# Moving the sample group's compressed branch and block ranking into the prompt attention's steps, and five buffers for its key and value units

## The chip, the cores and the metric

The kernel runs on one core of one Trainium2 chip. That core has five engines: TensorE (PE; its weight loads are shown apart as PEld), VectorE (DVE), ScalarE (ACT), GpSimd (POOL) and SyncE (SP), and 16 DMA engines that all queues share. The metric is the device time of one launch in microseconds. The kernel before takes 2581.03 us (median of three runs, 2580.56 to 2582.22).

## The reference

The reference is one inference step through two layers for two groups of tokens: a prompt of 512 tokens and a sample group of 8 sequences with 4 new tokens each, which have 2048 past tokens in 16 pages of a paged cache. Layer 0 mixes tokens by sparse attention in three branches, layer 1 by a Mamba-2 scan; each is followed by a SwiGLU. Cut to the attention of layer 0:

```python
lc = einsum(qg, kc) * scale - slopes * dist_c          # compressed branch: 127 blocks of the past
pc = masked_softmax(lc);  o_c = einsum(pc, vc)
imp = pad(pc.sum(heads of the group))                  # importance of the compressed blocks
p_slc = chunk sums of imp, 64 tokens a block           # 32 blocks of the past per query
score = where(forced, FORCE_SCORE, where(visible, p_slc, -1));  sel = top_k(score, 16)
ls = einsum(qg, k_sel) * scale - slopes * dist_s       # selected branch: only the chosen blocks
o_s = masked_softmax(ls) @ v_sel
o_w = windowed attention over the last 512 tokens      # window branch
o = gate0 * o_c + gate1 * o_s + gate2 * o_w;  y = o @ w_out;  x = x + y
```

The selected branch of the sample group can't be masked before the compressed branch has been ranked.

## The kernel before

All data is float32. SBUF is one hand-laid arena and PSUM eight banks of 512 columns. The program is a list of phases; each engine has its own instruction stream per phase, written out by hand with semaphores, and at the end of a phase all engines meet (`meet`). Nothing reorders the streams: the order in the code is the order on each engine.

Phase 3 (`p3_*`) is the prompt's attention. It walks 32 steps `s`: four query tiles `i` of 128 tokens, eight head pairs each. With tile `i` the keys have 128 (i+1) columns. In a step PE computes scores of step s (L1091, banks 0 to 3), turns the weights of step s-2 (L1109, banks 4 and 5), and multiplies values of step s-3 (L1129). DVE biases the scores of step s out of PSUM (`bias`, L1262), then scales the weights of step s-1 (`scale`, L1277). ACT takes the turned weights (L1192) and does the exponentials (L1184). The prompt's compressed branch for the next tile is inserted at steps k = 3 to 7 of each tile (`cmp_scores`, `cmp_bias`, `cmp_turn`). During phase 3 SP and POOL load the first key unit pair and the first value unit pair of the sample group, which then lie still.

Phase 4 (`p4_*`) is the sample group's attention. It treats the 8 sequences as four pairs. A unit is one sequence's selected keys or values: 16 pages of 128 KB, each one DMA whose source page is read from a table (`p4_load_unit`: page numbers into registers L1357, the DMAs L1360). There are four buffers for units: two for keys, two for values. SP loads the even sequence of a pair, POOL the odd one. The window is a 1 MB tile per sequence, keys and values in one DMA (L1380).

At its start phase 4 first copies the sample's queries into a block-diagonal form (L1536 to L1541), does the compressed scores of all pairs (L1393), their softmax on DVE and ACT, the importance (a product with `same_gt`, L1476, and the sums), and then ranks the 30 free blocks of each pair by comparing all with all: per pair five DVE instructions over 30x30 = 900 columns and a small one (L1567 to L1572). `sc_sel` is raised when the last pair is ranked. POOL waits for it and adds the chosen blocks' mask to the bias of 2048 columns (`comb`, L1621), SP waits for it before the second window tile, since the ranking's scratch lies there. PE waits for it before `turn(0)`.

Then PE runs, for each pair: `turn(pr)` (transposes of the weights, L1446), `scores(pr+1)` (L1405), `values(pr)` (L1458), `turn_out(pr)` (L1472), `win_scores(pr+1)` (L1421). DVE biases (L1590, L1592) once the mask of the pair is there, ACT does the exponentials (L1504, L1507), DVE sums the three branches (L1603 to L1605). SP's order in a pair: key unit after `ss_mm` (scores done), value unit after `ss_pv` (values done), then both window tiles after `ss_pv`. POOL's order: mask, key unit after `ss_mm`, value unit after `ss_pv`.

Phase 5 (`p5_*`) is the output projection: four units of seven products (L339), with weights in the four-slot ring, the first two of them needed at once. POOL forms sums of weight blocks (L385 to L392), and right before that issues one DMA that copies the whole window cache from DRAM to DRAM (`out_win`, L1629). The result is added to the residual `xT` (L1691), which stays in SBUF from the start of the kernel.

## Time and profile before

| | us |
|---|---|
| median of three runs | 2581.03 |
| the profiled execution, whole | 2581.04 |
| its span in the trace | 2579.6 |
| phase 3, the prompt's attention | about 610.1 to 836.65 |
| phase 4, the sample's attention | 836.65 to about 1046.4 |
| of it up to the last pair's ranking | 836.65 to 872.4 |
| ends of the pairs' value products | 904.3, 953.3, 1001.3, 1044.2 |

The whole execution is 1.4 us longer than its span. PE is busy 89% of the span. The times of phases are read off the timeline, by the first and last instruction of each. A busy DVE or PE in a stretch tells only that an instruction ran; the chain of waits tells which of them the end hung on.

### The profile page before, as it was taken

To read this page: it belongs to the slowest core of one execution; us is meant where nothing else is said; L and a number is where in the kernel's file an instruction comes from. 1 tells how busy PE (TensorE), PEld (TensorE's weight loads), DVE (VectorE), ACT (ScalarE), POOL (GpSimd) and SP (SyncE) were. 2 spreads that over 40 slices of the span, in tenths; PEclk is the share of its full clock that TensorE was granted. 3 is DMA by queue.
4 is the path that set the end of the run, shared out by engine and by line. 5 is a ranking of instruction groups with operands and counts; after the bars stand their busy time and mean duration, and the time that the engine had idled before them with its cause. 6 is when DMAs were issued, how large, how long until landed. Compare 5 with 4: busy or idle time off the path is not lost.

```text
span 2579.6 us, 34400 instructions
## 1 busy us (share of the span) xinstructions
PE 2288.9 (89%) x12318; PEld 1809.7 (70%) x12318; DVE 1284.4 (50%) x2112; ACT 513.9 (20%) x1205; POOL 785.0 (30%) x656
## 2 busy tenths in 40 slices
PE   7998999996788323899998999999877899999899
PEld 6866888775556211788886888788544687888687
DVE  5436333322566501555575226877667536557522
ACT  2101111113566111111110003232354001111000
POOL 4300000003000143534332424555364335433232
PEclk9988999996799665999999999999788899999999
DMA  4224333314000367521211221222132121121122
GB/s 157 83 77 126 98 99 98 86 54 141 3 1 4 125 202 266 202 82 66 98 66 45 90 112 68 71 83 84 69 129 99 53 95 66 66 98 66 47 89 80
DMA packets 86010, 234.92 MB, mean 91 GB/s; under 512 B 11121, under 2 KB 60402, under 8 KB 70610
## 3 DMA queue, kind: packets, MB, share of 16 engines
q1 hardware_dynamic: 78818, 202.84, 22.3%
q0 software_dynamic: 7024, 29.90, 3.5%
q8 instruction: 99, 1.62, 0.3%
q14 instruction: 69, 0.57, 0.1%
HBM read 216.23 MB, written 23.73 MB: 93 GB/s over the span
## 4 chain that ended last, share of the span: by engine, by line
PE 58%; DVE 9%; ACT 2%; issue 2%; SPq 2%; DMA 2%; POOL 2%; DVEq 0%; POOLq 0%; ACTq 0%
PE ps L339 46%; PE ps L1091 2%; DMA sbuf<-win 1%; PE ps L1129 1%; SPq L1360 1%; PE ps L1109 1%; POOL sbuf L2695 1%; PE ps L460 1%; ACT sbuf L1192 1%; ACT sbuf L1184 1%; PE ps L1458 1%; DVE sbuf L2078 1%; PE ps L1066 1%; DVE sbuf L2595 1%; PE ps L2268 1%
## 5 line engine op out<-in xcount | busy, mean ns | idle before, releaser
L339 PE MATMUL ps<-sbuf 128*128 128x272 f32 x6048 | 1406.5, 395 | 49.1 <-DVE sbuf L1836 19.4
L339 PEld LDWEIGHTS ps<-sbuf 128*128 128x128 f32 x6048 | 1156.4, 192 | 297.6 <-DVE sbuf L1836 20.3
L385 POOL TENSOR_TENSOR sbuf<-sbuf 128x512 f32<-128x512 f32 (+2 forms) x90 | 136.9, 1521 | 710.7 <-PE ps L339 631.1
L358 ACT ACTIVATE sbuf<-ps 128x272 f32<-128x272 f32 x180 | 71.5, 397 | 1104.4 <-PE ps L339 1075.4
L367 DVE TENSOR_TENSOR sbuf<-sbuf,ps 128x272 f32<-128x272 f32 x90 | 39.4, 438 | 246.4 <-PE ps L339 245.5
L392 POOL TENSOR_TENSOR sbuf<-sbuf 128x512 f32<-128x512 f32 (+2 forms) x90 | 145.2, 1613 | 8.1 <-PE ps L339 1.3
L389 POOL TENSOR_TENSOR sbuf<-sbuf 128x512 f32<-128x512 f32 (+2 forms) x90 | 140.0, 1556 | 7.1
L386 POOL TENSOR_TENSOR sbuf<-sbuf 128x512 f32<-128x512 f32 (+2 forms) x90 | 138.6, 1540 | 7.1
L788 PE MATMUL ps<-sbuf 128*128 128x256 f32 (+1 forms) x512 | 120.8, 387 | 2.9 <-DVE sbuf L905 2.9
L800 PE MATMUL ps<-sbuf 128*128 128x256 f32 (+1 forms) x512 | 120.0, 385 | 0.0
L794 PE MATMUL ps<-sbuf 128*128 128x256 f32 (+1 forms) x512 | 120.0, 385 | 0.0
L788 PEld LDWEIGHTS ps<-sbuf 128*128 128x128 f32 x512 | 95.2, 188 | 21.6 <-issue 4.8
L794 PEld LDWEIGHTS ps<-sbuf 128*128 128x128 f32 x512 | 96.2, 188 | 18.6
L800 PEld LDWEIGHTS ps<-sbuf 128*128 128x128 f32 x512 | 96.0, 188 | 18.6
L376 DVE TENSOR_TENSOR sbuf<-sbuf 128x272 f32<-128x272 f32 x90 | 105.5, 1172 | 3.1
L373 DVE TENSOR_TENSOR sbuf<-sbuf,ps 128x272 f32<-128x272 f32 x90 | 39.4, 438 | 131.1 <-PE ps L339 130.5
L945 DVE TENSOR_TENSOR sbuf<-sbuf,ps 128x256 f32<-128x256 f32 (+1 forms) x32 | 13.8, 430 | 180.3 <-PE ps L794 180.2
L369 DVE TENSOR_TENSOR sbuf<-sbuf,ps 128x272 f32<-128x272 f32 x90 | 39.3, 437 | 125.8 <-PE ps L339 125.0
L996 POOL DMA_DIRECT2D sbuf<-sbuf x16 | 9.8, 618 | 289.4 <-PE ps L788 273.0
L1421 PE MATMUL ps<-sbuf 128*32 128x512 f32 x32 | 7.7, 1058 | 99.4 <-DMA sbuf<-win 99.4
L1831 DVE TENSOR_TENSOR sbuf<-sbuf 128x544 f32<-128x544 f32 x88 | 93.0, 1056 | 3.0
L1262 DVE CUSTOM_DVE_ANT_0 sbuf<-ps,sbuf 128x128 f32<-128x128 f32 (+3 forms) x128 | 57.4, 490 | 52.1 <-PE ps L1091 47.6
(349 smaller groups left out, 2541.5 us busy)
## 6 DMA issues: line engine op xcount, KB each, us to landing
sbuf<-w_gu SPq DMA_DIRECT2D x44, 1024.0 KB, 5.9
sbuf<-cmp_pages SPq DMA_DIRECT2D x256, 128.0 KB, 2.3
sbuf<-w_down SPq DMA_DIRECT2D x32, 704.0 KB, 5.3
sbuf<-w_ssd_in SPq DMA_DIRECT2D x20, 1024.0 KB, 4.8
sbuf<-w_nsa_in SPq DMA_DIRECT2D x10, 1024.0 KB, 4.9
sbuf<-sel_k SPq DMA_DIRECT2D x64, 128.0 KB, 6.5
sbuf<-sel_k POOLq DMA_DIRECT2D x64, 128.0 KB, 5.6
sbuf<-sel_v SPq DMA_DIRECT2D x64, 128.0 KB, 4.3
```

What stands on the lines that cost most here:

```text
L339: last = pe.matmul(ps[:, bank_of(u, j), 0:HALF], a[:, kt * P:(kt + 1) * P], b[:, kt], start=kt == 0, stop=kt == kts - 1)
L358: do(act.activation(dst, bank_in(u, j), ACT.Copy), f_copied)
L376: do(dve.tensor_tensor(c1[:, n1], c1[:, n1], p4, ALU.add))
L385: do(pool.tensor_tensor(sv[:, 0], a21, a22, ALU.add), f_sums)
L386: do(pool.tensor_tensor(sv[:, 1], sv[:, 0], a11, ALU.subtract), f_sums)
L389: do(pool.tensor_tensor(sv[:, 2], a11, a21, ALU.subtract), f_sums)
L392: do(pool.tensor_tensor(sv[:, 3], a12, sv[:, 1], ALU.subtract), f_sums)
L788: last = pe.matmul(shared, ws[:, kt, hs], rows[:, kt, :, :, 1], start=kt == 0, stop=kt == KT - 1)
L794: last = pe.matmul(odd, w1(kv, 1, kt)[:, hs], e[:, kt], start=kt == 0, stop=kt == KT - 1)
L800: last = pe.matmul(even, w1(kv, 0, kt)[:, hs], d[:, kt], start=kt == 0, stop=kt == KT - 1)
L1262: dve.tensor_tensor_reduce(S_ring[:, n % S_BUFS, 0:w], ps[:, x, 0:w], cn_("dist")[:, SEQ - w:SEQ], -float(slope[head_of(gp * 4 + r, x % 2) ...
L1831: do(dve.tensor_tensor(c[:, x], c[:, x], rstd, ALU.mult), g_took if v % 2 == 0 else None)
```

## The change

Four edits go together.

1. The queries' copy, the compressed branch and the ranking move from the start of phase 4 into steps of phase 3. They use bank 4 between `turn(s-2)` and `values(s-3)` of a step, and the spent `xT` and parameter regions as scratch. The scores of the compressed branch are done at step 8, the exponential too, the weights on DVE at step 9, importance and block sums at step 10, the transposes at step 16, and the ranking in 16 parts at steps 12 to 27, four per pair. PE waits at `turn(s-1, 0)` of the next step until bank 4 has been read.
2. Units have five places (`a` to `e`), used in turn; `e` is `xT`. The first key unit of pair 1 is loaded in phase 3 (by SP, once the ranking is done).
3. PE does `values(pr)` and `turn_out(pr)` ahead of `scores(pr+1)`. SP loads a value unit after `ss_mm`, the window's key halves after `sw_mm`, its value halves after `ss_pv`, then the next key unit. POOL loads the odd key unit, then forms the mask, then loads the odd value unit.
4. `xT` is loaded again from DRAM at the start of phase 5, and DVE waits for it in unit 0. Two of the four weight slots are loaded after it, at `ss_pv` of the last pair; two after that of the third.

```diff
+        def sc_scores(pe, s):
+            sc_bank_free(pe, s)      # pe.wait_ge(a_pt, 4 * (s - 2) + 3)
+            pe.wait_ge(s_diag, 4)
+            for pr in range(PAIRS):
+                for bb, gp in QUARTERS:
...
+                    last = pe.matmul(ps[rows32(bb, gp), 4, pr * NC:(pr + 1) * NC], q_diag[gp][:, b], kcT[:, b, gp],
+        def sc_importance(pe, s):
...
+            pe.wait_ge(sc_dve, SC_DVE["weights"])
+            pe.matmul(ps[:, 4, 0:PAIRS * NC], cn_("same_gt"), weights_c.rearrange("p i n -> p (i n)"), start=True,
...
+        def sc_bias(dve, do):        # three instructions of 508 columns; sc_weights: four, one of them small;
+            dve.wait_ge(sc_pe, SC_PE["scores"])                # sc_blocks: three
...
+        def sc_rank(dve, do, pr, part):
...
+            if part == 0:
+                do(dve.tensor_tensor(above, other, mine, ALU.is_gt))
+            elif part == 1:
+                do(dve.tensor_tensor(equal, other, mine, ALU.is_equal))
+            elif part == 2:
+                dve.wait_ge(cn_in, 48)
+                do(dve.tensor_tensor(equal, equal, lower, ALU.mult))
+                do(dve.tensor_tensor(above, above, equal, ALU.add))
+            else:
+                do(dve.tensor_reduce(rank, above, AX.X, ALU.add))
+                do(dve.tensor_scalar(sel_bias[:, pr, 1:NBLK - 1], rank, TAKE - 0.5, NEG, ALU.is_gt, ALU.mult),
...
@@ p3_pe: turn(s, x)
+                if x == 0 and s + 1 == SC_SCORES:
+                    pe.wait_ge(sc_dve, SC_DVE["bank_read"])
+                if x == 0 and s + 1 == SC_IMPORTANCE:
+                    pe.wait_ge(sc_dve, SC_DVE["importance_read"])
...
@@ p3_dve, at the end of a step
+                if s == 4:
+                    sc_queries(dve, do)
+                if s == SC_SCORES:
+                    sc_bias(dve, do)
+                if s == SC_SCORES + 1:
+                    sc_weights(dve, do)
+                if s == SC_IMPORTANCE:
+                    sc_blocks(dve, do)
+                if SC_RANK <= s < SC_RANK + 4 * PAIRS:
+                    sc_rank(dve, do, (s - SC_RANK) // 4, (s - SC_RANK) % 4)
@@ p4_sp
+            p4_load_unit(sp, "K", 0)
+            p4_load_unit(sp, "V", 0)
+            sp.wait_ge(sc_dve, SC_DVE["blocks"])
+            sp.dma_start(lower.rearrange("p s o -> p (s o)"), t["const_n"][:, CONST_N["lower"]]).then_inc(cn_in, 16)
+            sp.wait_ge(sc_dve, SC_DVE["chosen"])
+            sp.wait_ge(sc_act, SC_ACT["turned_taken"])
+            p4_load_unit(sp, "K", 2)
...
+            sp.wait_ge(met, 12)
+            win_part(0, k_half, wk_in)
+            sp.dma_start(ali, t["const_ali"]).then_inc(late_in, 16)
+            rest = slice(CN_P3, CONST_N["lower"].start)
+            sp.dma_start(cn[:, rest], t["const_n"][:, rest]).then_inc(late_in, 16)
+            win_part(0, v_half, wv_in)
+            for pr in range(PAIRS - 1):
+                sp.wait_ge(ss_mm, pr + 1)
+                p4_load_unit(sp, "V", 2 * pr + 2)
+                sp.wait_ge(sw_mm, pr + 1)
+                win_part(pr + 1, k_half, wk_in)
+                sp.wait_ge(ss_pv, pr + 1)
+                win_part(pr + 1, v_half, wv_in)
+                if pr + 2 < PAIRS:
+                    p4_load_unit(sp, "K", 2 * pr + 4)
@@ p4_pe
             for pr in range(PAIRS):
                 turn(pr)
-                if pr + 1 < PAIRS:
-                    scores(pr + 1)
                 values(pr)
                 turn_out(pr)
                 if pr + 1 < PAIRS:
+                    scores(pr + 1)
                     win_scores(pr + 1)
@@ p4_pool
+            mask(0)
+            for pr in range(PAIRS - 1):
+                pool.wait_ge(ss_mm, pr + 1)
+                p4_load_unit(pool, "K", 2 * pr + 3)
+                pool.wait_ge(ss_s, pr + 1)
+                mask(pr + 1)
+                pool.wait_ge(ss_pv, pr + 1)
+                p4_load_unit(pool, "V", 2 * pr + 3)
@@ p5_sp
-            sp.wait_ge(ss_mm, PAIRS)
-            ring_rounds(sp, "nsa_out", 4)
+            sp.wait_ge(ss_pv, PAIRS - 1)
+            for i in range(2):
+                sp.dma_start(ring[:, (s0 + i) % RING], t["w_nsa_out"][i]).then_inc(w_in[(s0 + i) % RING], 16)
+            sp.wait_ge(ss_pv, PAIRS)
+            sp.dma_start(xT, t["x"]).then_inc(x_in, 16)
+            for i in range(2, 4):
+                sp.dma_start(ring[:, (s0 + i) % RING], t["w_nsa_out"][i]).then_inc(w_in[(s0 + i) % RING], 16)
```

## Rows read from the trace of the kernel before

**Rows 1.** Chain that ended last, by line, 836 to 1052 us.

```profile
by line: DMA sbuf<-win 16.4%; SPq L1360 12.5%; issue 10.6%; PE ps L1458 9.5%; SPq L1357 6.7%; PE ps L1405 6.6%; PE ps L1446 5.0%; DVE sbuf L1592 3.2%; DMA sbuf<-sel_k 3.0%; PE ps L1421 2.7%; DVE sbuf L1569 2.1%; DVE sbuf L1570 2.1%; DVE sbu
```

**Rows 2.** Stretches: length, busy per engine, granted PE clock, DMA share, GB/s.

```profile
694.00:836.65 142.65, 123.36 (x1148) 88.23 (x1148) 89.43 (x282) 95.17 (x265) 0.00 (x0) 0.96 0.01 1
836.65:872.40 35.75, 8.98 (x86) 3.88 (x86) 31.05 (x41) 1.23 (x2) 0.35 (x2) 0.64 0.21 81
904.30:953.30 49.00, 17.12 (x263) 10.55 (x263) 5.07 (x15) 6.80 (x15) 21.12 (x33) 0.62 0.64 215
```

**Rows 3.** The same chain in order of time (start, length), pair 1's cycle.

```profile
904.32 0.97 SPq L1357
...
918.94 12.56 DMA sbuf<-win
...
934.50 2.28 DVE sbuf L1592 x2
...
939.70 3.96 PE ps L1446 x17
943.66 4.43 PE ps L1405 x32
...
948.22 5.08 PE ps L1458 x184
```

**Rows 4.** Timeline of PE and DVE before and in the ranking.

```profile
844.31 2.06 PE L1476 MATMUL ps<-sbuf 128*128 128x508 f32 x2 [4.76 <-DVE sbuf L1552]
...
846.48 0.69 DVE L1557 COPY sbuf<-ps 128x508 f32<-128x508 f32 x1 [0.83 <-PE ps L1476]
...
848.91 1.10 DVE L1567 TENSOR_TENSOR sbuf<-sbuf 128x900 f32<-128x900 f32 x1
```

**Rows 5.** DVE, first bias of steps 9, 14, 17, 27; brackets: idle before.

```profile
677.13 0.43 DVE L1262 CUSTOM_DVE_ANT_0 sbuf<-ps,sbuf 128x256 f32<-128x256 f32 x1 [0.22 <-PE ps L1091]
...
709.28 0.43 DVE L1262 CUSTOM_DVE_ANT_0 sbuf<-ps,sbuf 128x256 f32<-128x256 f32 x1 [2.21 <-PE ps L1091]
...
724.67 0.56 DVE L1262 CUSTOM_DVE_ANT_0 sbuf<-ps,sbuf 128x384 f32<-128x384 f32 x1 [0.67 <-PE ps L1091]
...
792.58 0.69 DVE L1262 CUSTOM_DVE_ANT_0 sbuf<-ps,sbuf 128x512 f32<-128x512 f32 x1 [1.17 <-PE ps L1091]
```

**Rows 6.** Two stretches of 10 us, columns as in group 2.

```profile
690.00:700.00 10.00, 7.43 (x44) 5.72 (x45) 7.38 (x21) 3.51 (x11) 0.00 (x0) 0.67 0.00 0
...
1020.00:1030.00 10.00, 1.94 (x8) 0.23 (x8) 1.64 (x7) 0.45 (x1) 0.00 (x0) 0.50 1.02 417
```

**Rows 7.** POOL's timeline in pair 1: value unit, mask, key unit.

```profile
909.70 9.31 POOL L1360 DMA_DIRECT2D sbuf<-sel_v  x16 [22.21 <-issue]
919.03 3.63 POOL L1621 TENSOR_TENSOR sbuf<-sbuf 128x2048 f32<-128x2048 f32 x1
924.23 9.31 POOL L1360 DMA_DIRECT2D sbuf<-sel_k  x16 [1.58 <-issue]
```

**Rows 8.** DMA issues with median us to landing; the first of 836.6:872, then 904.3:953.

```profile
sbuf<-const_n SPq DMA_DIRECT2D x1, 770.0 KB, 6.3
...
sbuf<-win SPq DMA_DIRECT2D x2, 1024.0 KB, 11.1
sbuf<-sel_k POOLq DMA_DIRECT2D x16, 128.0 KB, 5.8
```

**Rows 9.** The copy `out_win`; a load issued beside it (1060.5); queues 1068:1072.

```profile
out_win<-win POOLq DMA_DIRECT2D x1, 28.5
...
sbuf<-w_gu SPq DMA_DIRECT2D x1, 1024.0 KB, 18.0
...
q0 software_dynamic: 16, 1.05, 77.0%
q1 hardware_dynamic: 16, 0.13, 9.1%
```

**Rows 10.** The chain after phase 4: all products of the output projection.

```profile
1052.31 51.86 PE ps L339 x224
```

More of the change, by code:

```diff
@@ L1006, in build @@
         top[0] = att_base
-        cn = region(CONST_N["own_head"].start)
+        cn = region(CONST_N["lower"].start)
         cn_ = lambda name: cn[:, CONST_N[name]]
@@ new lines, in sc_importance, with sc_turn @@
+        def sc_importance(pe, s):
+            sc_bank_free(pe, s)
+            pe.wait_ge(sc_dve, SC_DVE["weights"])
+            pe.matmul(ps[:, 4, 0:PAIRS * NC], cn_("same_gt"), weights_c.rearrange("p i n -> p (i n)"), start=True,
+                      stop=True).then_inc(sc_pe, 1)
+        def sc_turn(pe, s):
+            sc_bank_free(pe, s)
+            pe.wait_ge(sc_dve, SC_DVE["gated"])
+            for pr in range(PAIRS):
+                last = pe.transpose(ps[0:NC, 4, pr * P:(pr + 1) * P], Sc4[:, pr], ident)
+            last.then_inc(sc_pe, 1)
@@ L1332, in build @@
-        above = PT.rearrange("p j n -> p (j n)")[:, 512:512 + FREE_BLOCKS ** 2].rearrange("p (s o) -> p s o", s=FREE_BLOCKS)
-        equal = win[:, 1, 0:FREE_BLOCKS ** 2].rearrange("p (s o) -> p s o", s=FREE_BLOCKS)
-        dead_kv = kvT_flat[:, 0:8 * NT]
-        UNIT = [ring[:, 0:2].rearrange("p s n -> p (s n)"), ring[:, 2:4].rearrange("p s n -> p (s n)"),
-                hT_flat[:, 0:4096], dead_kv[:, 0:4096]]
-        K_of = [UNIT[b].rearrange("p (i g n) -> p i g n", i=NPAGE, g=2) for b in range(2)]
@@ L1338, in build, with place @@
-        V_of = [UNIT[2 + b].rearrange("p (i n) -> p i n", i=NPAGE) for b in range(2)]
+        dead_kv = kvT_flat[:, 0:8 * NT]
+        UNIT = {"a": ring[:, 0:2].rearrange("p s n -> p (s n)"), "b": ring[:, 2:4].rearrange("p s n -> p (s n)"),
+                "c": hT_flat[:, 0:4096], "d": dead_kv[:, 0:4096], "e": xT_flat[:, 0:4096]}
+        PLACE = {"K": (("a", "b"), ("e", "a"), ("d", "e"), ("c", "d")), "V": (("c", "d"), ("b", "c"), ("a", "b"), ("e", "a"))}
+        def place(kind, b):
+            return PLACE[kind][b // 2][b % 2]
@@ L1342, in build @@
-        win_in = [sem("win0_in"), sem("win1_in")]
+        unit_in = {(kind, b): sem(f"sel_{kind}{b}_in") for kind in "KV" for b in range(4)}
+        wk_in, wv_in = sem("win_k_in"), sem("win_v_in")
         win_stored = sem("win_stored")
-        s_diag = sem("q_diag_done")
-        sc_mm, sc_s, sc_e, sc_w, sc_imp, sc_t, sc_pt, sc_sel = [sem(f"sample_cmp_{n}") for n in (
-            "scores", "biased", "exp", "weights", "importance", "turned", "turned_taken", "selected")]
         s_comb = sem("sample_mask_done")
@@ L1360, in p4_load_unit @@
                 sp.dma_start(dst[:, i:i + 1], src[bass.ds(page, 1)].rearrange("o p n -> p o n")
-                             ).then_inc(unit_in[x], 16)
+                             ).then_inc(unit_in[kind, b % 4], 16)
         def p4_sp(sp):
             sp.wait_ge(w_used, slot_at["w1"] + 4)
-            for pr in range(PAIRS):
-                for x in (0, 2):
-                    if pr >= 1:
-                        sp.wait_ge(ss_mm if x < 2 else ss_pv, pr)
-                    p4_load_unit(sp, x, 2 * pr)
-                if pr == 0:
-                    sp.wait_ge(met, 12)
-                    sp.dma_start(ali, t["const_ali"]).then_inc(late_in, 16)
-                    rest = slice(CN_P3, CONST_N["lower"].stop)
-                    sp.dma_start(cn[:, rest], t["const_n"][:, rest]).then_inc(late_in, 16)
-                for b in range(2):
-                    if pr >= 1 and b == 0:
-                        sp.wait_ge(ss_pv, pr)
-                    if pr == 0 and b == 1:
-                        sp.wait_ge(sc_sel, 1)
-                    sp.dma_start(win[:, b], t["win"][2 * pr + b]).then_inc(win_in[b], 16)
+            p4_load_unit(sp, "K", 0)
@@ L1397, in scores @@
             def scores(pr):
-                for x in range(2):
-                    pe.wait_ge(unit_in[x], 16 * NPAGE * (pr + 1))
+                for bb in range(2):
+                    pe.wait_ge(*unit_there("K", 2 * pr + bb))
                 if pr >= 1:
@@ L1472, in turn_out @@
                 pe.transpose(ps[:, 7, 0:P], o_rows, ident).then_inc(ss_ot, 1)
-            pe.wait_ge(sc_w, 1)
-            pe.matmul(ps[:, 6, 0:PAIRS * NC], cn_("same_gt"), weights_c.rearrange("p i n -> p (i n)"), start=True,
-                      stop=True).then_inc(sc_imp, 1)
-            pe.wait_ge(sc_w, 2)
-            for pr in range(PAIRS):
-                last = pe.transpose(ps[0:NC, 7, pr * P:(pr + 1) * P], Sc4[:, pr], ident)
-            last.then_inc(sc_t, 1)
             scores(0)
@@ L1688, in p5_dve @@
                 sum_products(dve, dve_do, U_NSA_OUT + i, seven_regs, c[:, 0], c[:, 1])
+                if i == 0:
+                    dve.wait_ge(x_in, 32)
                 for x in range(2):
```

201 lines of the change are left out of this document (108 added, 93 removed).

## The prediction

> **What bounds the kernel now.** I read four views, in this order. The first is the chain that ended last in the stretch of the sample's attention [rows 1]. Its largest shares are no arithmetic: 16.4% waits for window data, 12.5% is SP issuing DMAs (L1360), 6.7% is SP reading page numbers (L1357). The stretches say the same: from 904.3 to 953.3, one pair, PE is busy 17.12 of 49 us and VectorE 5.07, and the DMA engines move 215 GB/s; in the first 35.75 us VectorE is busy 31.05 us and PE 8.98 [rows 2]. So the stage has two parts with different limits, 35.7 us of the compressed branch and ranking on VectorE, then four pairs paced by a queue. The third view, the chain in order of time, shows how a pair is paced [rows 3]: after the values SP reads page numbers, issues 16 value pages and only then the window (904.32 to 918.94, 14.6 us), the window lands 12.56 us later, and only then come window scores, bias (2.28), exponential, turns (3.96), scores of the next pair (4.43) and values (5.08). The fourth is VectorE's timeline in the prompt's steps, which says how much room the moved work finds [rows 5].
>
> **The change part by part, phase 4.** I count from the start of phase 4, which lies at 836.65. Before, the last pair's values end at 1044.2, so at 207.6.
>
> *Pair 0.* Key units of pair 0 are there, so its scores end at about 6 (5 us and a start). The mask waits for constants: key halves, `ali` and the rest are 2.33 MB, where before 1.75 MB had landed 6.7 us after the start (issue 0.4 us in, 6.3 us to land [rows 8]); 0.58 MB more at the 417 GB/s of a full stretch [rows 6] is 1.4 us, so 8.1. Mask 3.63 [rows 7] gives 12 with POOL's start. VectorE's two small biases and 2.28 of L1592 give 15.5, the exponential 2.2 more, 17.8. Turns, with the last take, 4.6; 22.4. Values 5.08 [rows 3]: 27.7. The four pairs' first values before ended at 67.7 (904.3). This removes the ranking (35.7) and the wait for pair 1's key unit, which held up values(0) because its scores came first.
>
> *Pairs 1 to 3.* Two cycles compete. The arithmetic of a pair: sum of branches and `turn_out` 2, scores 4.4 to 5.7 (5.5 taken), window scores 2, biases 3.1, exponential 2.2, turns 4.5, values 5.2: 24.6 us [rows 3]. POOL's queue: it reads page numbers for 5.4 us (904.32 to 909.70), issues for 9.31, the mask takes 3.63, and the next unit's page numbers are read beside the mask, as before (mask at 919.03, first DMA at 924.23, 5.2 us later) [rows 3, 7]. In the new order that is key unit 14.6, mask and value unit 14.5: 29.1 us for a pair. A page lands 5.8 us after its issue [rows 8]. Laid out: first key unit of POOL (K3) issued 13.5 to 22.8, landed 28.5, in time for scores(1) at 29.7; its value unit V3 starts at values(0) done, 27.7, and lands at 48; turns(1) are done at 46.6, so values(1) run 48 to 53.2. K5 is issued 47.6 to 56.9 and lands at 62.5: scores(2) wait for it from 55. Values(2) end at 84.9. K7 is issued 76.6 to 85.9 and lands at 91.5: scores(3) wait again, 91.5 to 97; then 2, 3.1, 2.2, 4.5 and 5.2 give values(3) done at **114**. SP issues 13 to 14 us for a unit, two units and four window halves a pair, 29 us too, but each of its transfers is wanted later than POOL's, and I give it nothing. The window, which paced the stage, lands ahead: its key halves for pair 2 are issued at about 57 for window scores at 68, against 11.1 us to land [rows 8].
>
> The stage gives back 207.6 - 114 = **93.6 us**. Bounds: if POOL's queue didn't count, 27.7 + 3 x 24.6 = 101.5 (gain 106); if the unit landings in the two waits and the window's were all as slow as the 11.1 us of a window tile, another 5 on each of two waits and on one value unit, 129 (gain 79). I take the layout by rows, nearer to the first since 31 MB in 114 us are 290 GB/s, below the 417 of a full stretch [rows 6].
>
> **Phase 3, what is added.** A step here is a loop of scores, bias, turns and values, in which VectorE's idle time before the next bias says what fits. At steps 8 to 10 it is 0.22 us or less [rows 5]: nothing fits. Step 8: PE's compressed scores take 1.1 and VectorE waits for them, then three instructions of 0.71 over 508 columns; the next bias starts at 679.8 for 677.13, +2.65. Step 9: 3 x 0.71 + 0.2 = +2.4. Step 10: importance is 2.06 on PE [rows 4], VectorE waits, three of 0.71 follow, +3.1. Sum 8.1. The four query copies at step 4 (1.0) lie in an idle gap behind the prompt's compressed branch: 0.
> The ranking's parts are 1.13, 1.13, 2.26 and 1.32 us (L1567 is 1.10 [rows 4]). At steps 12 to 15 and 20 to 23 the gaps are 1.8 to 3.1 (one of 2.21 stands in [rows 5]), since the prompt's own inserts hold PE: only about 0.6 remains, where step 19's part sits in front of step 20's bias. The gap that step 16 leaves is 0.67, the two after it are 0.41 and 0.73, the one of step 26 is 1.17 [rows 5]: the excess is 0.5 + 0.7 + 1.5 + 0.3 (step 25) + 1.1 = 4.1. The transposes at step 16 (four of about 0.27 on PE and a take on ScalarE) are not hidden, PE leads there: 1.2. Sum 5.9. The clock: PE's granted clock was 0.67 in the 10 us after the prompt's own inserted work [rows 6], which is a mean over stretches at 1.2 and at 2.4 GHz. Inserted VectorE work makes PE idle in the same way at steps 8 to 10, so I add 2 us, two steps at the lower level, each about 1 us longer. Phase 3: **+16**. Bounds: nothing below 8 (steps 8 to 10 have no cover), and 36, if no added instruction found room (31 on VectorE, 4 on PE, 1 on ScalarE).
>
> **Phase 5, what is moved.** Before, all four weight slots were issued at 1015.9, 28 us ahead of the last values. Now `xT` (2.2 MB) and slots 2 and 3 are issued when values(3) end, and 2.4 us later POOL issues the window copy. Beside that copy a 1 MB load took 18.0 us to land, and in 1068 to 1072 the software queue moved 1.05 MB and the hardware queue 0.13 [rows 9]. So little passes until the copy lands, 28.5 us after its issue [rows 9]. About 0.8 MB go ahead of it, `xT` lands some 22 us after the last values, slot 2 at 35, slot 3 at 37. `xT` was first used 18 us after them, but VectorE may be late there while PE has banks free. A product is 51.86 / 28 = 1.85 us [rows 10], a unit 13 us, so PE wants slot 2 at 30.3 and slot 3 at 43: a stall of **+5**. Bounds 0 (the copy starts later or gives way) and 12 (all of `xT` waits for the copy, then slot 2).
> The Trainium skill's page "DMA: Bandwidth & Descriptors", section "Queues, rings and completion order", says each DMA engine takes turns between its queues, one packet at a time. The trace agrees in kind: 16 packets each, 1.05 MB against 0.13. By that rule with 17 KB packets of `xT` the stall is the one above; by the page's fit of 2 us plus bytes at 436 GB/s, which knows no second queue, it would be nought and the time 5 us less.
>
> **Sum.** Profiled execution 2581.04 (0.01 from the median): 2581.0 - 93.6 + 16 + 5 = 2508.4. I forecast **2508 us**.
>
> **The rivals.**
> *A: POOL's queue isn't late.* Units land sooner or arithmetic is slower than thought, and pairs take 24.6 us: 101.5 for 114, so 2496. For it: waits at K5 and K7 of only 7 and 5 us. Against: POOL's 9.31 us were the same in both units shown. 13%.
> *B: The two queues hold each other up.* SP's and POOL's units overlap nearly all the time now, each at some 225 GB/s (128 KB in 0.58 us [rows 7]), together above the 417 of [rows 6]; landings as slow as 11.1 us: 129 for 114, and 2523. 13%.
> *C: The ranking finds no room.* VectorE's parts delay bias, exponentials and takes in turn, and phase 3 grows by 36, not 16: 2528. Against: idle gaps of over 2 us in eight of sixteen steps. 7%.
> *D, the other side: the clock.* If VectorE's inserts let PE idle so that it is granted 1.2 GHz through steps 8 to 31, its 123.4 busy us [rows 2] up to double. That costs up to 105 and, with the 2 us above taken out, the kernel ends at 2611. It decides, against the gain of 73, from 70% of these steps at the lower level. Against: the clock was back at full after such a drop within 20 us, three times. 2%.
> *E: The window copy gives way*, the stall of phase 5 is 0 and the rest as forecast: 2503; it lies in the forecast's own range.
>
> **How the numbers follow.** The forecast with E has 65%, A 13%, B 13%, C 7%, D 2%. The range to leave out 2 in 10 takes in A's and B's centres and ends before their far sides: 2490 to 2528. A measurement of this kernel can tell 0.2%, 5 us, from no change. All cases but D are faster by 50 us or more; for mechanisms I haven't seen I leave 2% for no change and 3% for slower with D's share in it. Faster 95%.
>
> **What would show it.** Right: phase 3 longer by 16, half of it at steps 8 to 10; phase 4's first instruction a 512-column score, first values done 28 us in, last at 114; PE waiting for `sel_k` pages of POOL before scores(2) and scores(3), and no wait for `win`; a wait of some 5 us for a slot at output unit 2. Wrong: pairs longer than 32 us with SP in the chain; granted clock below 0.9 over steps 12 to 31; phase 3 growing by more than 25.

## The result, and the profile after

| | before | after |
|---|---|---|
| median, us (range) | 2581.62 (2580.56 to 2587.92, 4 runs) | 2513.71 (2511.26 to 2515.15, 4 runs) |
| ratio, 95% interval | 1 | 0.9731 (0.9713 to 0.9749) |
| profiled execution; its span | 2581.04; 2579.6 | 2514.76; 2512.8 |
| phase 3, its first PE instruction to the start of phase 4 | 226.6 | 244.0 |
| phase 4 start to last values | 207.6 | 115.6 |
| ends of the pairs' values, from its start | 67.7, 116.7, 164.7, 207.6 | 29.0, 57.0, 88.2, 115.6 |
| last values to the first product of the next stage (L460) | 59.8 | 65.7 |

The kernel is 67.9 us faster, 2.7%. The forecast was 2508, the range 2490 to 2528. The spans differ by 66.8 us, and the table accounts for it: -92.0 in phase 4, +17.5 in phase 3, +5.9 behind the last values; +1.4 come from the stages ahead of phase 3 and +0.4 from those behind L460, which the change does not touch. The start of phase 3 lies between 609.9 and 612.7 us in all the traces here, whichever kernel runs, so these two are no effect of the change.

The first view of the kernel after is the same as [rows 2], one stretch for each pair and two behind them: length, busy time and count for PE, PEld, DVE, ACT, POOL, granted PE clock, share of the DMA engines, GB/s.

```profile
855.50:884.40 28.90, 15.37 (x262) 10.33 (x262) 4.08 (x12) 6.15 (x11) 16.37 (x20) 0.76 0.89 303
884.40:911.00 26.60, 15.76 (x220) 11.19 (x223) 5.07 (x15) 6.81 (x15) 15.16 (x28) 0.74 0.80 264
911.00:940.00 29.00, 16.21 (x195) 9.79 (x191) 5.08 (x15) 6.81 (x15) 21.59 (x35) 0.71 1.05 357
940.00:971.00 31.00, 20.14 (x391) 13.80 (x383) 5.07 (x15) 6.81 (x15) 14.41 (x21) 0.83 0.80 291
971.00:979.20 8.20, 6.05 (x18) 4.31 (x18) 6.87 (x7) 0.95 (x5) 5.54 (x4) 0.79 0.96 374
```

VectorE's 31.05 us at the start of the stage [rows 2] are gone (4.08 in the first stretch). PE is busy 15.4 to 20.1 us in a pair's stretch (17.12 before), DVE the same 5.07, but in 27 to 31 us instead of 49, and the DMA engines move 264 to 357 GB/s, not 215. The arithmetic did not get shorter; what stood around it did.

The waits in phase 4 (engine and line, what it waited for, us in total, times, longest) say what is late now:

```profile
PE ps L1543 <- DMA sbuf<-sel_k: 7.6, 2, 5.5
...
PE ps L1591 <- DMA sbuf<-sel_v: 6.3, 2, 4.2
...
PE ps L1556 <- DMA sbuf<-win: 1.9, 1, 1.9
```

The window, 16.4% of the chain in [rows 1], costs 1.9 us. In its place are key and value units. POOL's timeline (start, length, instruction, count, idle before) shows whose:

```profile
904.22 9.32 POOL L1500 DMA_DIRECT2D sbuf<-sel_k  x16 [5.09 <-issue]
913.55 3.62 POOL L1701 TENSOR_TENSOR sbuf<-sbuf 128x2048 f32<-128x2048 f32 x1
918.37 5.22 POOL L1500 DMA_DIRECT2D sbuf<-sel_v  x9 [1.19 <-issue]
...
932.79 9.31 POOL L1500 DMA_DIRECT2D sbuf<-sel_k  x16 [4.80 <-issue]
942.12 3.63 POOL L1701 TENSOR_TENSOR sbuf<-sbuf 128x2048 f32<-128x2048 f32 x1
949.37 9.31 POOL L1500 DMA_DIRECT2D sbuf<-sel_v  x16 [3.63 <-issue]
```

POOL has hardly a gap but the reading of page numbers: 932.79 - 904.22 = 28.6 us from key unit to key unit, forecast 29.1. Only the last idle time, 3.63 us for 1.19 a pair earlier, is longer, since that value unit had to wait for values(2). All four waits of PE end within 0.3 us of the landing of the last page of a unit of POOL's (904.65, 919.42, 947.21 and 965.46); SP's units had landed before. PE's timeline in the same two pairs (of before: the durations in [rows 3]):

```profile
919.51 5.47 PE L1543 MATMUL ps<-sbuf 128*32 128x512 f32 x32 [5.54 <-DMA sbuf<-sel_k]
...
947.30 5.23 PE L1543 MATMUL ps<-sbuf 128*32 128x512 f32 x32 [2.06 <-DMA sbuf<-sel_k]
...
955.46 0.63 PE L1567 MATMUL ps<-sbuf 128*128 128x128 f32 x4 [1.95 <-ACT sbuf L1625]
...
959.64 3.98 PE L1578 MATMUL ps<-sbuf 128*128 128x128 f32 x17 [3.44 <-ACT sbuf L1635]
965.74 5.23 PE L1591 MATMUL ps<-sbuf 127*32 127x128 f32 x184 [2.12 <-DMA sbuf<-sel_v]
...
973.24 5.62 PE L339 MATMUL ps<-sbuf 128*128 128x272 f32 x16 [0.70 <-ACTq L251]
979.10 22.27 PE L339 MATMUL ps<-sbuf 128*128 128x272 f32 x96 [0.25 <-DVE sbuf L399]
1005.52 6.80 PE L339 MATMUL ps<-sbuf 128*128 128x272 f32 x22 [4.14 <-DMA sbuf<-w_nsa_out]
```

Scores(2) and scores(3) wait for `sel_k`, as forecast (the second only 2.06 us), and values(1) for `sel_v`, 4.2 us. One wait was not forecast: values(3) wait 2.12 us for a value page. That unit is itself late by the values before it: values(2) end at 943.65, POOL reads the page numbers for 5.7 us (first DMA 949.37), issues until 958.7, the last page lands at 965.5. The last line above is the forecast stall of the output projection: 4.14 us at slot 2, 34.5 us behind the last values (forecast 35), and PE had wanted it at 30.4 (forecast 30.3).

DVE's timeline at steps 8 to 10 of phase 3, the counterpart of [rows 5], shows in three places the instructions of the compressed branch and behind them the bias of the next step, with no idle time in the first two and 0.59 us in the third. Here they stand between steps 8 and 9:

```profile
679.00 0.69 DVE L1117 TENSOR_TENSOR sbuf<-ps,sbuf 128x508 f32<-128x508 f32 x1 [0.45 <-PE ps L1079]
679.73 0.68 DVE L1119 TENSOR_REDUCE sbuf<-sbuf 128x4 f32<-128x508 f32 x1
680.44 0.69 DVE L1120 TENSOR_TENSOR sbuf<-sbuf 128x508 f32<-128x508 f32 x1
681.16 0.42 DVE L1391 CUSTOM_DVE_ANT_0 sbuf<-ps,sbuf 128x256 f32<-128x256 f32 x1
```

Where phase 3 grew, read off the first scores of each step (period of a step, us):

| step | 8 | 9 | 10 | 11 | 12 | 13 | 14, 15 | 16 | 17, 18 | 19 | 20 | 21 | 22 to 31 |
|---|---|---|---|---|---|---|---|---|---|---|---|---|---|
| before | 3.1 | 3.1 | 3.5 | 10.8 | 9.4 | 5.4 | 5.4 | 4.4 | 4.4, 4.8 | 12.5 | 7.9 | 6.9 | as after |
| after | 4.9 | 3.8 | 8.3 | 13.1 | 9.0 | 6.0 | 5.4 | 6.0 | 4.4, 4.8 | 13.8 | 11.4 | 7.9 | as before |

### The profile page after: what moved, and what is told of

Its sections match the earlier page's. It is cut to its first block, busy times and chain, and to the rows that moved or that the text cites. A ratio compares the mean times of both kernels' runs of the same rounds, so it can differ in the third digit from the quotient of the medians.

```text
span 2512.8 us, 34405 instructions
## 1 busy us (share of the span) xinstructions
PE 2300.0 (92%) x12318; PEld 1822.5 (73%) x12318; DVE 1280.1 (51%) x2109; ACT 514.7 (20%) x1205; POOL 786.6 (31%) x660
## 4 chain that ended last, share of the span: by engine, by line
PE 57%; DVE 8%; issue 3%; ACT 2%; POOL 2%; DMA 2%; POOLq 1%; DVEq 0%; ACTq 0%; SPq 0%
PE ps L339 47%; PE ps L1204 1%; DMA sbuf<-w_nsa_out 1%; PE ps L1248 1%; ACT sbuf L1309 1%; PE ps L460 1%; PE ps L1228 1%; ACT sbuf L1317 1%; DVE sbuf L2171 1%; POOL sbuf L2788 1%; PE ps L1179 1%; POOLq L1497 1%; PE ps L2413 1%; DVE sbuf L2681 1%; PE ps L2361 1%
## 5 line engine op out<-in xcount | busy, mean ns | idle before, releaser
L367 DVE TENSOR_TENSOR sbuf<-sbuf,ps 128x272 f32<-128x272 f32 x90 | 39.4, 437 | 248.3 <-PE ps L339 247.4
L794 PEld LDWEIGHTS ps<-sbuf 128*128 128x128 f32 x512 | 96.2, 188 | 18.6
L800 PEld LDWEIGHTS ps<-sbuf 128*128 128x128 f32 x512 | 96.0, 188 | 18.6
L945 DVE TENSOR_TENSOR sbuf<-sbuf,ps 128x256 f32<-128x256 f32 (+1 forms) x32 | 13.8, 430 | 181.9 <-PE ps L794 181.9
L373 DVE TENSOR_TENSOR sbuf<-sbuf,ps 128x272 f32<-128x272 f32 x90 | 39.4, 437 | 130.7 <-PE ps L339 130.1
L369 DVE TENSOR_TENSOR sbuf<-sbuf,ps 128x272 f32<-128x272 f32 x90 | 39.4, 437 | 125.8 <-PE ps L339 125.0
L1924 DVE TENSOR_TENSOR sbuf<-sbuf 128x544 f32<-128x544 f32 x88 | 92.9, 1056 | 3.0
L365 DVE TENSOR_TENSOR sbuf<-sbuf,ps 128x272 f32<-128x272 f32 x90 | 39.4, 438 | 83.5 <-PE ps L339 67.7
```

What stands on the lines that cost most here:

```text
L794: last = pe.matmul(odd, w1(kv, 1, kt)[:, hs], e[:, kt], start=kt == 0, stop=kt == KT - 1)
L800: last = pe.matmul(even, w1(kv, 0, kt)[:, hs], d[:, kt], start=kt == 0, stop=kt == KT - 1)
L1924: do(dve.tensor_tensor(c[:, x], c[:, x], rstd, ALU.mult), g_took if v % 2 == 0 else None)
```

## The experiments

All ratios are against the kernel before on the same chip. "Values" are the ends of the pairs' value products, counted from the start of phase 4. The phases are read off one trace of each kernel, and such readings differ between traces: phase 4 has the same instructions up to its last values in the kernel after, e1, e3 and e10, and they end at 115.6, 118.0, 118.2 and 121.3. A difference of 3 us in that column tells nothing by itself.

| run | median us | ratio (95%) | phase 3 | values | last values to L460 |
|---|---|---|---|---|---|
| after | 2513.71 | 0.9731 (0.9713 to 0.9749) | 244.0 | 29.0, 57.0, 88.2, 115.6 | 65.7 |
| e1_copy_early | 2508.73 | 0.9714 (0.9695 to 0.9733) | 240.6 | 29.4, 56.8, 87.7, 118.0 | 59.7 |
| e2_pages_ahead | 2513.69 | 0.9739 (0.9716 to 0.9761) | 241.5 | 30.3, 52.6, 84.8, 116.1 | 67.1 |
| e3_no_rank | 2515.15 | 0.9732 (0.9714 to 0.9750) | 241.0 | 29.4, 56.9, 86.5, 118.2 | 67.8 |
| e4_scores_first | 2556.07 | 0.9891 (0.9870 to 0.9911) | 244.0 | 40.7, 87.4, 132.9, 158.8 | 66.7 |
| e5_combined | 2505.23 | 0.9688 (0.9674 to 0.9702) | 241.5 | 30.2, 53.8, 83.9, 114.4 | 59.7 |
| e6_pool_one_dma | 2524.38 | 0.9767 (0.9752 to 0.9781) | 241.0 | 29.8, 55.0, 98.5, 124.3 | 66.6 |
| e7_before_no_rank | 2560.96 | 0.9916 (0.9897 to 0.9935) | 226.5 | 47.1, 94.6, 144.1, 187.4 | 59.7 |
| e8_before_values_first | 2566.94 | 0.9929 (0.9914 to 0.9944) | 226.6 | 61.0, 104.4, 149.3, 194.0 | 59.7 |
| e9_half_bytes | 2500.57 | 0.9678 (0.9662 to 0.9695) | 244.0 | 29.6, 52.7, 78.2, 111.6 | 59.7 |
| e10_no_branch | 2500.14 | 0.9680 (0.9664 to 0.9696) | 227.7 | 30.7, 59.0, 89.6, 121.3 | 68.2 |

**e1_copy_early.** The window copy is issued in phase 3.

```diff
@@ p3_pool, after the value unit
+            pool.dma_start(t["out_win"], t["win"]).then_inc(win_stored, 16)
@@ p5_pool
-            pool.dma_start(t["out_win"], t["win"]).then_inc(win_stored, 16)
```

> The window cache's DRAM-to-DRAM copy is issued in phase 3, after GpSimd's second value unit, where the DMA engines are nearly idle, instead of at the start of phase 5. Theory (the copy starves the reload of xT and the last two weight slots): after the last values, slot 2 lands in about 12 us for 34.5, PE has no wait before output unit 2, the stretch from the last values to the end of the four output units is 60 us for 65.9, and the kernel takes about 6 us less than the changed kernel: 2507.5. Rival (the reload is late by its own bytes, 4.3 MB behind the last values): slot 2 lands no sooner than 25 us after the last values, and the time changes by under 2 us. A second rival: the copy in phase 3 delays what is loaded there and phase 3 grows by as much as is saved.

The stretch behind the last values is 59.7 us long, as in the kernel before. The third weight slot (slot 2) lands 11.1 us after the last values, for 34.5 in the kernel after. The timeline of PE, against the last three lines of the kernel after above, has no wait for a slot:

```profile
970.62 3.93 PE L340 MATMUL ps<-sbuf 128*128 128x272 f32 x16 [0.70 <-ACTq L252]
976.49 33.73 PE L340 MATMUL ps<-sbuf 128*128 128x272 f32 x146 [1.94 <-DVE sbuf L400]
```

So the copy is the cause of the phase 5 stall, and all 6 us go with it: 4.14 of waiting, and 1.7 in the 22 products right behind the wait, which took 6.80 us where 22 of the 146 above take 5.1. The granted clock was 0.77 in those 6.8 us of the kernel after and 1.00 in the 22 us before the wait. (The first 16 products, 5.62 us for 3.93, cost nothing: the next product begins 5.87 us behind the first in both.) The median gains 5.0 us, though the intervals of the two ratios overlap; the stretch in the trace is the firmer reading. The DMA view of the kernel after in that stretch (971 to 1010: packets, MB, share of the engines; then issues with us to landing; the last two lines are the queues from 980 to 990, amid the copy) shows how it came:

```profile
q0 software_dynamic: 144, 8.39, 57.9%
q1 hardware_dynamic: 618, 5.73, 39.3%
...
sbuf<-x SPq DMA_DIRECT2D x1, 2176.0 KB, 13.9
sbuf<-w_nsa_out SPq DMA_DIRECT2D x2, 1024.0 KB, 35.1
...
out_win<-win POOLq DMA_DIRECT2D x1, 31.3
...
q0 software_dynamic: 56, 3.67, 98.9%
q1 hardware_dynamic: 53, 0.33, 10.5%
```

The copy moves 58 KB a packet, SP's loads 9.3 KB, and both wait in the same engines. This is the rule of the Trainium skill's page "DMA: Bandwidth & Descriptors", section "Queues, rings and completion order", by which a DMA engine alternates between its queues one packet at a time. The trace agrees: amid the copy the two queues moved 56 and 53 packets, but 3.67 and 0.33 MB.

**e4_scores_first and e8_before_values_first.** One puts PE's old order into the kernel after, the other the new order into the kernel before.

```diff
@@ e4: p4_pe                     |  @@ e8: p4_pe of the kernel before (side by side)
+  if pr + 1 < PAIRS:            |  -  if pr + 1 < PAIRS:
+      scores(pr + 1)            |  -      scores(pr + 1)
   values(pr)                    |     values(pr)
   turn_out(pr)                  |     turn_out(pr)
   if pr + 1 < PAIRS:            |     if pr + 1 < PAIRS:
-      scores(pr + 1)            |  +      scores(pr + 1)
       win_scores(pr + 1)        |         win_scores(pr + 1)
```

> PE's order in a pair is put back: turns, scores of the next pair, values, turn_out, window scores; all else as changed. Theory (edit 3's order matters since scores(pr+1) wait for GpSimd's key unit while values(pr) could run, and the values release the next value unit): each pair's values end after the landing of the next key unit, about 8 us later in pair 0 and each later cycle is GpSimd's value unit, key unit, mask in one chain with the landing, about 34 us; last values at 130 us for 115.5, kernel 2528. Rival (the order is of no weight now that one key unit lies ready): under 3 us.

> The kernel before with PE's order of the change alone: values(pr) and turn_out(pr) ahead of scores(pr+1). Four buffers, SyncE's order and the ranking stay. Theory (in the kernel before the next scores took 4.4 us ahead of the values in each of three cycles, and in pair 0 they also waited 4.1 us for a key unit, all of it ahead of the SyncE queue that paced the pair): each of the three cycles starts 4.4 us sooner, pair 0 another 4, last values at about 190 us for 207.6, kernel 2564. Rival, from the 43 us that the order is worth in the changed kernel: the order alone brings most of it here too, 40 us and more. Second rival: the scores now in the chain after the values cost what they cost before, and nothing is gained.

The order is worth 43 us in the kernel after (158.8 for 115.6), where 15 were expected, and 13.6 in the kernel before, where 17.6 were. The reason is a closed loop, which the two timelines of e4 show, POOL's and then PE's:

```profile
900.57 9.31 POOL L1500 DMA_DIRECT2D sbuf<-sel_v  x16 [17.66 <-issue]
914.98 9.31 POOL L1500 DMA_DIRECT2D sbuf<-sel_k  x16 [5.09 <-issue]
```

```profile
893.75 1.39 PE L1591 MATMUL ps<-sbuf 128*32 128x128 f32 x44
...
930.20 6.48 PE L1543 MATMUL ps<-sbuf 128*32 128x512 f32 x32 [22.37 <-DMA sbuf<-sel_k]
...
936.61 5.21 PE L1591 MATMUL ps<-sbuf 127*32 127x128 f32 x184
```

Values end at 895.1; POOL then reads page numbers (5.4), issues the value unit (9.3), reads again (5.1), issues the key unit (9.3); it lands 5.9 us later; scores take 6.4 and only behind them come the values, whose weights had been turned by 907.8. The sum is 41.5 + 5.2 = 46.7 us, and the first cycle of e4 is 87.4 - 40.7 = 46.7. All three cycles waited so: PE's waits for `sel_k` are 51.3 us in e4, for 7.6 in the kernel after. With values first the loop is open: values(pr) no longer stand behind a key unit that their own predecessor released. In the kernel before this order gains little since the window, issued behind a whole value unit [rows 3], comes last in any case (the cycles of e8 are 43.4, 44.9 and 44.7, and PE waits 87.6 us for `win` in its phase 4). The parts don't add up one by one: without the order the rest of the change takes the last values from 207.6 to 158.8, and the order then takes 43.2 more. No run takes away the five places, the halved window or the new order of SP and POOL by itself, so what each of these is worth within the 92 us is not shown.

**e7_before_no_rank.** The ranking's comparisons are taken out of the kernel before.

```diff
@@ p4_dve
-  # the five comparisons over 900 columns and the threshold, for each pair
+  do(dve.memset(sel_bias[:, pr, 1:NBLK - 1], 0.0), sc_sel if pr == PAIRS - 1 else None)
```

> The kernel before with the ranking's comparisons left out (a memset of the mask in their place, so no block is masked out); the rest of the compressed branch stays at the start of phase 4. Theory (the ranking is wholly on the path there: SyncE's second window tile and the next key unit, GpSimd's mask and PE's turns all wait for it): the first values end 21 to 23 us sooner, at 45 to 47 us after the start of phase 4 for 68, later cycles stay at 48 us, kernel 2559. Rival (the window and unit transfers, which could start sooner only by contending, hold pair 0 anyway): less than 15 us gained.

The first values end 20.6 us earlier and the last 20.2, and the median gains 0.84%, some 21.7 us. VectorE's ranking took 23.4 us (848.91 to 872.34), and the four memsets in its place take 0.6. The ranking was on the path for nearly all of its length, and nothing later takes it back.

**e3_no_rank and e10_no_branch.** Both start from the kernel after. e3 leaves out the 16 ranking parts, e10 everything of the compressed branch and the ranking.

```diff
@@ e3: sc_rank
+  if part == 3:
+      dve.wait_ge(cn_in, 48)
+      do(dve.memset(sel_bias[:, pr, 1:NBLK - 1], 0.0), sc_dve if pr == PAIRS - 1 else None)
+  return
@@ e10: p3_pe, p3_act, p3_dve
-  # sc_scores, sc_importance, sc_turn, sc_exp, sc_take, sc_bias, sc_weights, sc_blocks, sc_rank and their waits
...
+  if s == 28:
+      dve.wait_ge(cn_in, 48)
+      do(dve.memset(few_c[:, 0], 0.0), sc_dve)
```

> The ranking's five instructions over 900 columns per pair are left out of the prompt's steps and a memset of the mask stands in their place, so no block of the past is masked out; the compressed branch stays. Theory A (the ranking costs where VectorE's idle time before a bias is short: steps 16 to 18 and 25, 26): phase 3 is 4 us shorter, spread over those steps. Theory B, from the trace of the changed kernel, where steps 17, 18 and 24 to 27 are as long as before and steps 19 to 21 are 5.8 us longer with a lower granted clock: the ranking costs only beside the prompt's own inserted branch, and phase 3 is about 5 to 6 us shorter, all of it in steps 19 to 21. Theory C: those steps are longer for another reason, the phase of the clock, and nothing is gained.

> The changed kernel with all of the sample's compressed branch and ranking left out of phase 3 (scores, softmax, importance, transposes, comparisons); the query copies, the memsets and the constants' load stay, its weights are zero and no block is masked. Theory (the whole growth of phase 3, 17.5 us from its first to its last instruction, is steps 8 to 11, step 16 and lower clock behind them; the ranking is hidden, as e3 showed): phase 3 takes 227 us as in the kernel before, steps 8 to 10 3.1, 3.1, 3.5 us again, phase 4 unchanged, kernel 2496. Rival (the new memsets, the copies at step 4 or the other layout cost part of it): phase 3 stays 3 us or more above 226.6.

Without the ranking phase 3 takes 241.0 us. With it it takes 240.6 in e1, 241.0 in e6, 241.5 in e2 and e5, and 244.0 in the kernel after, e4 and e9. Steps 12 to 18 and 22 to 30, where 13 of the 16 parts stand, have the same periods in e3 as in the kernel after, to 0.1 us. So no cost of the ranking is seen, neither there nor beyond the 3.4 us by which the traces with it differ among themselves. Those 3.4 us lie in step 11 (10.4 or 13.1 us, at a granted clock of 0.83 or 0.63) and in steps 20 and 21 (9.3 and 6.9 us against 11.4 and 7.9). Here are the stretches 750 to 760, 760 to 770 and 770 to 780 of the kernel after, and then of e1, whose instructions there are the same and run some 2 us sooner:

```profile
750.00:760.00 10.00, 8.96 (x62) 8.62 (x64) 4.99 (x13) 2.74 (x9) 0.00 (x0) 0.66 0.01 2
760.00:770.00 10.00, 5.98 (x44) 4.24 (x42) 8.65 (x22) 5.48 (x15) 0.00 (x0) 0.81 0.00 1
770.00:780.00 10.00, 8.55 (x70) 5.79 (x68) 4.84 (x14) 4.47 (x13) 0.00 (x0) 0.85 0.01 2
```

```profile
750.00:760.00 10.00, 9.94 (x59) 8.39 (x58) 4.46 (x10) 1.46 (x4) 0.00 (x0) 0.52 0.00 0
760.00:770.00 10.00, 7.18 (x64) 4.65 (x61) 8.84 (x25) 5.40 (x16) 0.00 (x0) 0.97 0.00 1
770.00:780.00 10.00, 7.51 (x76) 5.36 (x76) 7.87 (x22) 7.54 (x24) 0.00 (x0) 1.00 0.01 2
```

The granted clock falls in both, but in one it is back at 0.97 after 760 and in the other at 0.81; over step 20 it is 0.85 and 0.79. e10 has 227.7, so everything inserted costs 244.0 - 227.7 = 16.3 us, 13 to 14 of it without the slower return of the clock, and the 1.1 us between e10 and the kernel before are within such differences (its step 20 takes 9.7). In e10 phase 4 is longer (121.3), though its code is the same: in the last pair PE waits 6.3 us for the window, where the kernel after has no such wait. Why the window came later was not pursued.

**e2_pages_ahead.** Page numbers are read before the wait, for POOL's units and SP's value units.

```diff
 def p4_load_unit(sp, kind, b, *wait):
     ... page numbers into registers
+    if wait:
+        sp.wait_ge(*wait)
@@ p4_pool
-  pool.wait_ge(ss_mm, pr + 1)
-  p4_load_unit(pool, "K", 2 * pr + 3)
+  p4_load_unit(pool, "K", 2 * pr + 3, ss_mm, pr + 1)
...  # the same for POOL's value unit and SP's value unit
```

> GpSimd reads the page numbers of each unit ahead of the wait for the place, not after it (SyncE likewise for its value units). The same DMAs in the same order. Theory (GpSimd's queue paces pairs 2 and 3): its first value unit of phase 4 starts 5 us after the wait is met before and at once now, key and value units follow up to 5 us earlier, the waits for sel_k and sel_v pages in phase 4 (7.6 and 6.3 us in the changed kernel) shrink, and the last values end 4 to 6 us sooner: about 110.5 us after the start of phase 4 for 115.5, kernel 2509. Rival (bytes pace it: the DMA engines were 1.05 busy from 911 to 940): landings stretch as issues come sooner, under 1.5 us gained.

Pair 1 ends 4.4 us earlier and pair 2 3.4, but the last pair 0.5 later; the median doesn't move, so the 4 to 6 us expected did not come. The waits of phase 4 show what took it back, 5.8 us for the window against 1.9 us in the kernel after:

```profile
PE ps L1544 <- DMA sbuf<-sel_k: 7.2, 2, 5.2
...
PE ps L1557 <- DMA sbuf<-win: 5.8, 3, 2.8
```

SP's queue is as full as POOL's: the window's key halves stand behind its value unit, and those of pairs 2 and 3 are issued 58.9 and 89.0 us into the phase, for 58.3 and 89.1 in the kernel after, while PE comes for them 4 and 2 us sooner.

**e5_combined.** e1 and e2 together (SP's value unit without a wait of its own), and SP issues the window's key halves ahead of the value unit.

```diff
@@ p4_sp
-  sp.wait_ge(ss_mm, pr + 1)
-  p4_load_unit(sp, "V", 2 * pr + 2)
   sp.wait_ge(sw_mm, pr + 1)
   win_part(pr + 1, k_half, wk_in)
+  p4_load_unit(sp, "V", 2 * pr + 2)
```

> Both correct edits of the first batch, and SyncE issues the window's key halves of the next pair before its value unit, not after it: copy early (worth 6.4 us in the trace), page numbers ahead on GpSimd, window first. Theory (with page numbers ahead GpSimd runs 5.5 us sooner by pair 3 and only the window key halves, queued behind SyncE's value unit, took its place as the last to land): last values end 110 us after the start of phase 4, for 115.5 and 116.1, no wait for win before window scores, kernel about 2503. Rival (the DMA engines are full in pairs 2 and 3, so whoever is issued first only delays another): last values at 114 us or later, with a wait for sel_v or sel_k in place of win, kernel 2507 to 2508.

2505.2 us, the fastest of the versions that compute everything: 8.5 us, 0.34%, below the kernel after, and the intervals of the two ratios do not meet. 5 of them are e1's copy; the other 3.5 (118.0 to 114.4 for the last values) are within what the traces and intervals leave open, so the window's new place is not shown to gain. The last values at 114.4 are what the rival expected. The last two cycles are still 30.1 and 30.5 us, and the stretch of one of them has the DMA engines full:

```profile
906.00:937.00 31.00, 19.09 (x272) 12.36 (x271) 5.14 (x16) 6.80 (x15) 23.47 (x37) 0.72 1.05 355
```

**e9_half_bytes.** Are the last cycles bound by bytes or by issue? e5 with pages of 64 KB (128 of 256 columns) from pair 1 on.

```diff
+  n = 256 if b < 2 else 128
-  sp.dma_start(dst[:, i:i + 1], src[bass.ds(page, 1)]...
+  sp.dma_start(dst[:, i:i + 1, 0:n], src[bass.ds(page, 1), :, 0:n]...
```

> The kernel of e5 with the same DMAs at the same places in the queues, but each page of a unit from pair 1 on carries 128 of its 256 columns (64 KB for 128): half of the heads' keys and values of these pairs are left out, what lay in the place before is used. A pair then moves 6.3 MB for 10.5. Theory (bytes bound pairs 2 and 3 in e5: 10.5 MB in 30.3 us are 346 GB/s with the engines over 1.0 busy): the two last cycles, 30.1 and 30.5 us in e5, fall to 25 to 27, near the 24.6 of arithmetic; last values at 104 to 107 us for 114.4. Rival (the queues' issuing bounds them: 29.1 us of GpSimd, 28 of SyncE a pair, whatever a page holds): cycles of 29 to 30 us, last values at 112 or later.

The stretches of the last three pairs, and POOL's timeline in the last cycle:

```profile
884.00:911.00 27.00, 17.98 (x344) 12.40 (x336) 6.07 (x18) 6.97 (x17) 18.79 (x34) 0.87 0.68 206
911.00:940.00 29.00, 16.44 (x263) 11.83 (x263) 5.07 (x15) 7.17 (x19) 21.55 (x34) 0.79 0.71 213
```

```profile
915.39 5.21 POOL L1504 DMA_DIRECT2D sbuf<-sel_v  x9 [1.20 <-issue]
...
929.79 9.29 POOL L1504 DMA_DIRECT2D sbuf<-sel_k  x16 [4.81 <-issue]
939.09 3.62 POOL L1704 TENSOR_TENSOR sbuf<-sbuf 128x2048 f32<-128x2048 f32 x1
944.21 9.28 POOL L1504 DMA_DIRECT2D sbuf<-sel_v  x16 [1.49 <-issue]
```

With 40% fewer bytes and the engines at 0.7, POOL needs 944.21 - 915.39 = 28.8 us for a pair, as before, and the last values end at 111.6 for 114.4, between the theory's 104 to 107 and the rival's 112. The middle cycle falls to 25.5, about the 24.6 of the arithmetic, and the last rises to 33.4, since the queue had fallen behind: their mean is 29.5 for 30.3. So the queue of issues sets the pace. The 2.8 us that the bytes may add in three pairs are no more than what traces of the same phase 4 differ by.

**e6_pool_one_dma.** POOL's units of pairs 1 to 3 as one DMA of 2 MB each, from 16 pages in a row at fixed places instead of the table's.

```diff
+  if b % 2 and b > 1:
+      sp.dma_start(dst, src[b * NPAGE:(b + 1) * NPAGE].rearrange("o p n -> p o n")).then_inc(unit_in[kind, b % 4], 16)
+      return
...  # and the counts that PE waits for
```

> GpSimd's units of pairs 1 to 3 are one 2 MB DMA each from fixed consecutive pages, not from the 16 pages of the table, so these sequences attend to other keys and values; the bytes are the same, while GpSimd's 5.4 us of page numbers and 9.3 us of issue per unit go. Theory (GpSimd's queue paces pairs 2 and 3): its units land about 7 us after their release, waits for sel pages of GpSimd's go, pairs take 25 to 27 us, last values at 106 to 109 us for 115.5; kernel 2506. Rival (bytes and SyncE's queue, which also needs 29 to 31 us a pair, are as tight): last values at 113 us or later.

It is slower than the kernel after, though POOL is busy only 1.15 us with a unit, not 9.3, and reads no page numbers. The longest wait of PE moved to the window:

```profile
PE ps L1561 <- DMA sbuf<-win: 23.9, 3, 18.6
```

In a stretch of phase 4 the software queue now moves 4.0 KB a packet (4.19 MB in 1056) where the kernel after has 2.7 (4.20 in 1538), against 1.2 to 1.3 on SP's. The large transfers take 14 to 15 us to land and SP's window halves 12.7, for 7.8 in the kernel after. SP's queue falls behind as well: its key unit of pair 2 takes 12.4 us to issue for 9.0. Of the 18.6 us that the window scores of pair 2 stand, 3.3 pass until SP, busy with its value unit, issues the key halves (915.57), and the rest is their landing, 14.0 us for the second where it took 8.3 in the kernel after. With that landing the wait would still have been some 13 us. So POOL's quicker units gain little because SP's queue comes next, and larger transfers beside it make it later still. That the packets are the cause was not isolated: the big DMA also starts all its bytes at once.

## Why the prediction was right, step by step

*Pair 0 and the ranking* (27.7 forecast, 29.0 measured). e7 shows that the ranking was on the path, for 20.6 of its 23.4 us.

*Pairs 1 to 3* (53.2, 84.9, 114 forecast; 57.0, 88.2, 115.6 measured). The bound named was POOL's queue, with 29.1 us a pair: it has 28.6, PE's waits end with its landings, and e9 shows that it holds when the bytes are cut. Three details of the layout were off. The last cycle was laid out over the key unit; it ran over the value unit: from values(2) to values(3) 5.7 + 9.3 + 6.8 + 5.2 = 27.0 and a start. Pair 1 came 3.8 us late: values(0) were 1.3 late and with them POOL's value unit, which landed at 49.2 for 48; the products then took 7.5 us for 5.2, at a granted clock of 0.68 (those of pair 2 took 7.0). And SP's queue, to which the forecast gave nothing, held the window back for 1.9 us once; e2 and e6 show that it is the next bound, close behind. The layout's 31 MB in 114 us are 272 GB/s, not 290; the argument from it stands the better.

*The order of PE* was in the layout and not priced by itself. By e4 43 of phase 4's 92 us hang on it, through a loop of which the prediction names only the wait in pair 0. There the total is right for a reason that the prediction gives only in part.

*Phase 3* (+16 forecast, +17.5 measured, 16.3 by e10). Steps 8 to 10 are right: the three biases came 2.6, 2.2 and 3.2 us later, 8.0 in all for 8.1. The term of 4.1 for the ranking at steps 16 to 18, 25 and 26 is wrong: those steps kept their periods, and e3 finds no cost. The rule "DVE idle before the bias is the room" was too strict there. A likely reason, which no run isolates, is that the bias of a step need only be done before PE wants its weights, a step or more later. Two readings behind it were slightly off, without weight for the sum: the idle time after step 10 is 0.29 us, and seven gaps, not eight, are over 2 us. The transposes at step 16 cost 1.6 for 1.2. What filled the sum was steps 11, 19, 20 and 21, which grew by 2.3, 1.3, 3.5 and 1.0, 8.1 in all, where 2 for the clock and 0.6 had been allowed. Steps 11, 20 and 21 are those in which runs of the same instructions differ by the clock (10.4 for 13.1 us in step 11 of e1 and e6). So 4.1 too much for the ranking and 5.5 too little for these steps nearly cancelled: that phase 3 came out at +17.5 for +16 is in part luck. In the traces where the clock came back sooner it grew by only 14 to 15.

*Phase 5* (+5 forecast, +5.9 measured). Wait, place and cause are as forecast, slots 2 and 3 land at 34.5 and 37.3 us for 35 and 37, and e1 takes all of it away. `xT` landed at 14.0, not 22: SP's packets were of 9.3 KB on average, not 17. The 1.7 us beyond the stall of 4.14 are the products right behind it at a lower clock, a term that the sum did not have.

*The rivals.* A (the queue not late, 24.6 us a pair): the pairs took 28.0, 31.2 and 27.4 us, with 13.9 us of waits for POOL's units, and e9's queue keeps its pace with fewer bytes. B (129 for 114) did not come, though the engines are full in one pair (357 GB/s). C (ranking without room, +36) did not come either, and e3 finds no cost. D (1.2 GHz through steps 8 to 31): the granted clock was 0.93 over steps 12 to 31, and steps 22 to 31 have the periods of before. E (the copy gives way): it does not.

Of the 6.4 us between the sum, 2508.4, and the profiled execution, 2514.8, 1.6 are in phase 4, 1.5 in phase 3, 0.9 in phase 5 and 1.4 ahead of phase 3; 1.0 is left, outside the span and at its end. None is larger than the 3.4 us by which phase 3 alone differs between traces.

## What to carry to other kernels

Draw the loops of waits, not only the queue's length: an order on PE that puts a consumer behind a unit which its own release starts closes a loop over read, issue, landing and arithmetic, and cost 43 us here. Inserted work costs where the engine that it goes to holds up the step (VectorE at steps 8 to 10, 8 us); where another engine does, it may cost nothing, even if the gap ahead of the next instruction is shorter than the work. When a queue that issues many small DMAs is the bound, fewer large ones need not help: here the other queue was nearly as full, and its loads landed later beside them. A copy nobody waits for is best issued where no load is wanted.
